# Forgetting attention on one Trainium2 core: scores from three split single-pass products instead of fp32 matmuls

## The reference, cut to what matters

```python
def forgetting_attention(q, k, v, f_pre, q_g, k_g):
    q = jnp.moveaxis(rms_norm_2(q, q_g), 1, 2)
    k = jnp.moveaxis(rms_norm_2(k, k_g), 1, 2)
    F = cumsum(log_sigmoid(f_pre))
    # for each block of 128 queries:
    logits = einsum('bhqd,bhkd->bhqk', q_blk, k) * Dh ** -0.5 + (F_q - F_k)
    logits = where(k_pos <= q_pos, logits, -inf)
    out = softmax(logits) @ v
```

## Time and profile before

| | |
|---|---|
| median of 3 runs | 1962.59 us (1961.63 to 1962.9) |
| the profiled execution | 1962.23 us |
| its span, first to last instruction | 1960.4 us |
| PE busy | 1946.3 us, 99% |
| VectorE, ScalarE, GpSimd busy | 45%, 39%, 31% |
| granted TensorE clock | 1.0 throughout |
| a pair of heads in the attention stage, from one to the next | 26.87 us (6 pairs in the steady rhythm) |

### The profile page before, as it was taken

The page is one execution under the profiler, slowest core; times in us unless marked ns, Lnnn a source line. Parts: engine busy times, 40 slices in busy tenths (PEclk is TensorE's granted clock), DMA queues, the critical chain, the costliest instruction groups (busy, mean ns, idle before and its releaser), DMA issues. The chain is left out here.

```text
span 1960.4 us, 26570 instructions
## 1 busy us (share of the span) xinstructions
PE 1946.3 (99%) x9186; PEld 1562.1 (80%) x9186; DVE 891.8 (45%) x1446; ACT 770.7 (39%) x1199; POOL 603.3 (31%) x238
## 2 busy tenths in 40 slices
PE   9999999999999999999999999999999999999999
PEld 7777888888888888888877887777788888888887
DVE  6888663344534544355274445555221364222200
ACT  7444442222222422222256556666422344222211
POOL 0000124444442344444403330000344423444443
PEclk9999999999999999999999999999999999999999
DMA  4111235555422455543212222222233333333322
GB/s 168 54 54 55 76 118 193 192 193 186 146 92 86 155 193 192 194 170 134 87 59 85 66 86 86 86 75 75 66 96 96 97 97 97 96 96 96 110 92 98
DMA packets 59271, 220.25 MB, mean 112 GB/s; under 512 B 6592, under 2 KB 7360, under 8 KB 59216
## 3 DMA queue, kind: packets, MB, share of 16 engines
q1 hardware_dynamic: 59216, 219.55, 34.0%
HBM read 217.39 MB, written 2.13 MB: 112 GB/s over the span
## 5 line engine op out<-in xcount | busy, mean ns | idle before, releaser
L438 POOL TENSOR_TENSOR wlo<-raw,whi 128x1024 fp32r<-128x1024 f32 (+1 forms) x234 | 603.0, 2577 | 1343.4 <-ACT whi L956 1343.4
L479 PE MATMUL bank<-xh,whi 128*128 128x512 f32 x1632 | 645.5, 396 | 3.5 <-DVE wlo L1512 3.3
L479 PE MATMUL bank<-xh,wlo 128*128 128x512 f32 x1632 | 635.8, 390 | 0.0
L479 PE MATMUL bank<-xl,whi 128*128 128x512 f32 x1632 | 635.5, 389 | 0.0
L956 ACT ACTIVATE whi<-raw 128x1024 fp32r<-128x1024 f32 (+1 forms) x298 | 330.2, 1108 | 604.4 <-PE bank L479 580.5
L479 PEld LDWEIGHTS bank<-xh,whi 128*128 128x128 f32 x1632 | 306.4, 188 | 81.4 <-issue 14.4
L479 PEld LDWEIGHTS bank<-xh,wlo 128*128 128x128 f32 x1632 | 306.3, 188 | 64.8
L479 PEld LDWEIGHTS bank<-xl,whi 128*128 128x128 f32 x1632 | 306.6, 188 | 62.3 <-issue 1.0
L479 PE MATMUL bank<-acth,whi 128*128 128x512 f32 x528 | 205.7, 390 | 1.4 <-POOL wlo L438 1.4
L1932 DVE SCALAR_TENSOR_TENSOR adaw<-adaw,crow 128x1024 f32<-128x1024 f32 x72 | 107.6, 1495 | 218.4 <-DMA adaw<-ada_dram 218.4
L479 PE MATMUL bank<-acth,wlo 128*128 128x512 f32 x528 | 205.4, 389 | 0.0
(11 more groups left out here) (314 smaller groups left out, 2017.1 us busy)
## 6 DMA issues: line engine op xcount, KB each, us to landing
raw<-w_dram SPq DMA_DIRECT2D x250, 512.0 KB, 3.6
adaw<-ada_dram SPq DMA_DIRECT2D x72, 512.0 KB, 4.3
raw<-wd_dram SPq DMA_DIRECT2D x48, 704.0 KB, 4.0
adaw<-w_dram SPq DMA_DIRECT2D x8, 512.0 KB, 4.4
norms<-fox_log_decays SPq DMA_DIRECT2D x8, 512.0 KB, 4.4
h<-x_dram SPq DMA_DIRECT2D x4, 512.0 KB, 6.9
out_dram<-h SPq DMA_DIRECT2D x8, 256.0 KB, 4.3
crow<-w_dram SPq DMA_DIRECT2D x2, 512.0 KB, 6.2
```

What stands on the lines that cost most here:

```text
L438: nc.gpsimd.tensor_tensor(wlo[:, s, 0:width], raw[:, s, 0:width], whi[:, s, 0:width].bitcast(F32), ALU.subtract).then_inc(sem("w_lo"), 1)
L479: mm = nc.tensor.matmul(proj[b][:], w[:, s, W], v[:, k, :], start=first and j == 0 and a == 0, stop=last and j == len(chunks) - 1 and a == ...
```

## The change

It does four things.

1. `fox_scores` computes scores from split operands. `fqq[:, e]` holds the high part of head e's queries twice, in both halves of the rows; `fkk[:, e]` holds the high part of its keys in its own half and the low part in the other half. One fp32r matmul over all 128 rows per head gives high-by-high plus high-by-low, and a second one over the head's 64 rows adds the low part of the queries (`fql`) by the high part of the keys. Low by low is left out. The mask is unchanged.
2. `fox_normed` writes its result over `fraw`. ScalarE makes the high parts in six copies of 64 partitions (`fox_high`), VectorE the low parts in four subtractions of 64 partitions (`fox_low`). `fox_high` stands in ScalarE's list between the roots and `split` of slab s+3. `f_qk` now counts six signals: four from VectorE and the two last copies of ScalarE.
3. The scores of the next pair's block 0 move behind chunks 3 to 6 of slab s+2 on PE; at the start they move behind two more chunks of slab 3.
4. On VectorE `weight_low` of slab s+3 moves from before the maxima of the next pair's block 0 to behind their scaling.

`fql` lies in the space of `gates_raw`, which is used earlier.

```diff
-        fq = sb("fq", [P, 2, S], F32, fox)
-        fk = sb("fk", [P, 2, S], F32, fox)
+        fqq = sb("fqq", [P, 2, S], F32R, fox)
+        fkk = sb("fkk", [P, 2, S], F32R, fox)
+        fql = low_part[:, 8:8 + S]
...
-        BESIDE = (((0, 0, 6),), ((0, 6, 8), (1, 0, 5)), ((1, 5, 8), (2, 0, 3)), ((2, 3, 8),))
+        BESIDE = (((0, 0, 6),), ((0, 6, 8), (1, 0, 5)), ((1, 5, 8), (2, 0, 3)), ((2, 3, 7), (2, 7, 8)))
...
                 if b == 0:
-                    pe.wait_ge(sem("f_qk"), primed(t * 2 + 2))
+                    pe.wait_ge(sem("f_qk"), primed(t * 6 + 6))
                 for e in range(2):
-                    H = slice(e * DH, e * DH + DH)
-                    nc.tensor.matmul(bank[2 + e][:, 0:W], fq[H, tt, b * P:W], fk[H, tt, 0:W], start=True, stop=False,
+                    nc.tensor.matmul(bank[2 + e][:, 0:W], fqq[:, e, b * P:W], fkk[:, e, 0:W], start=True, stop=False,
+                                     skip_group_check=True)
+                for e in range(2):
+                    H = halves(e)[0]
+                    nc.tensor.matmul(bank[2 + e][:, 0:W], fql[H, b * P:W], fkk[H, e, 0:W], start=False, stop=False,
                                      skip_group_check=True)
...
-                    elif more:
-                        fox_scores(t + 1, 1 - tt, 0)
...
+                            if (j, lo) == (2, 7):
+                                fox_scores(t + 1, 1 - tt, 0)
                             wide("fox", i, 6, s + j, part=(lo, hi))
...
-            wide("fox", 0, 6, 3, part=(0, 4))
+            wide("fox", 0, 6, 3, part=(0, 6))
             pe.wait_ge(sem("m_gated"), primed(MH * 2))
             fox_scores(0, 0, 0)
-            wide("fox", 0, 6, 3, part=(4, KC))
+            wide("fox", 0, 6, 3, part=(6, KC))
...
+            def fox_high(p):
+
+                act.wait_ge(sem("f_normed"), p * 2 + 1)
+                act.wait_ge(sem("scores"), p * 8 + UA)
+                for e in range(2):
+                    H = halves(e)[0]
+                    nc.scalar.activation(fkk[H, e, :], fraw[H, 1, :], ACT.Copy).then_inc(sem("f_hi"), 1)
+                act.wait_ge(sem("f_normed"), p * 2 + 2)
+                for e in range(2):
+                    H = halves(e)[0]
+                    nc.scalar.activation(fqq[H, e, :], fraw[H, 0, :], ACT.Copy).then_inc(sem("f_hi"), 1)
+                for e in range(2):
+                    H, O = halves(e)
+                    nc.scalar.activation(fqq[O, e, :], fraw[H, 0, :], ACT.Copy).then_inc(sem("f_qk"), 1)
...
                         fox_root(t + 1, 1)
                         fox_root(t + 1, 0)
+                        fox_high(t + 1)
                         split(i, 6, SLAB["fox"], s + 3, WC)
...
+            def fox_low(p):
+
+                for e in range(2):
+                    H, O = halves(e)
+                    dve.wait_ge(sem("f_hi"), p * 4 + (e + 1))
+                    V.tensor_tensor(fkk[O, e, :], fraw[H, 1, :], fkk[H, e, :].bitcast(F32), ALU.subtract).then_inc(sem("f_qk"), 1)
+                for e in range(2):
+                    H = halves(e)[0]
+                    dve.wait_ge(sem("f_hi"), p * 4 + (e + 3))
+                    V.tensor_tensor(fql[H, :], fraw[H, 0, :], fqq[H, e, :].bitcast(F32), ALU.subtract).then_inc(sem("f_qk"), 1)
...
                     for j in (1, 0):
                         fox_normed(t + 1, 1 - tt, j)
-                    weight_low(i, 6, s, 3)
+                    fox_low(t + 1)
                     fox_maxima(t + 1, 1 - tt, 0)
                     fox_maxima(t + 1, 1 - tt, 1)
                     fox_scale(t + 1, 0)
                     fox_scale(t + 1, 1)
+                    weight_low(i, 6, s, 3)
```

More of the change, by code:

```diff
@@ L114, in build @@
         leb = sb("leb", [P, P], BF16)
-        gates_raw = sb("gates_raw", [P, KC * 96])
+        grs = ExitStack()
+        gates_raw = sb("gates_raw", [P, KC * 96], F32, grs)
+        grs.close()
+        low_part = sb("low_part", [P, KC * 96], F32R)
         stat = sb("stat", [P, 2, 8])
@@ L1351, in fox_tile @@
                 matmuls(i * 6 + (SLAB["fox"] + s + 1))
-                act.wait_ge(sem("f_qk"), primed(p * 2))
+                act.wait_ge(sem("f_qk"), primed(p * 6))
                 bias = c1("b_fox", i * 6 + s)
@@ L1457, in _ @@
                 fox_root(0, j)
+            fox_high(0)
             fox_values(0, 2)
@@ L2169, in fox_normed @@
                 dve.wait_ge(sem("f_rstd"), p * 2 + (2 - j))
-                V.scalar_tensor_tensor((fq, fk)[j][:, par, :], fraw[:, j, :], c1(("fox_q", "fox_k")[j], p), frs[:, j, :], ALU.mult,
-                                       ALU.mult).then_inc(sem("f_qk"), 1)
+                V.scalar_tensor_tensor(fraw[:, j, :], fraw[:, j, :], c1(("fox_q", "fox_k")[j], p), frs[:, j, :], ALU.mult,
+                                       ALU.mult).then_inc(sem("f_normed"), 1)
+            def fox_low(p):
[7 more added lines that the diff above has]
+                    V.tensor_tensor(fql[H, :], fraw[H, 0, :], fqq[H, e, :].bitcast(F32), ALU.subtract).then_inc(sem("f_qk"), 1)
             def fox_pair(i, tt, more=True):
@@ L2201, in _ @@
                 fox_normed(0, 0, j)
+            fox_low(0)
             for k in range(2):
```

## The result

| | before | after |
|---|---|---|
| median | 1962.28 us (6 runs, 1961.45 to 1962.9) | 1971.93 us (6 runs, 1971.46 to 1973.84) |
| profiled execution | 1962.23 us | 1971.99 us |
| its span | 1960.4 us | 1970.2 us |

The ratio of the times is 1.0052, with a 95% interval from 1.0043 to 1.0062. The change makes the kernel 9.65 us slower: slower by more than 0.2%, as forecast, 1.5 us above the predicted time and within the range.

What follows compares the result with a forecast made beforehand. PE's list was taken as the bound, busy 1946.3 of 1960.4 us. From 1962.23, −3.5 (PE's gain) + 8.3 (stall) + 3.1 (first pair) gave 1970.1, against the median 1970.4 us, slower by 0.4%; range 1965 to 1974.

Steps and rivals of the forecast that it cites:

- The bound and the number on which it turns: PE's list bounds the kernel; `fox_values(t, 1)` starts 3.13 us after the block 3 `fpT` copies it needs.
- ScalarE's six copies: Ahead of split and `fpT` copies: 0.41 us wait plus six at 0.63, 3.78, making them 4.19 us later.
- The 0.12 that I added: Delay in us from the end of ScalarE's last `fpT` copy until PE sees it, at 1239.63.
- the stall's term: PE waits for `fpT` before the values, 1.18 us in each of 7 pairs: +8.3 us.
- No overlap between copies that change the half: Copies alternating partition half, like the two 64-partition squares, don't overlap on ScalarE: 0.63 us each.
- The threshold of that rival: Rival: copies overlap, 0.52 us each, sum +2.6, 1965.2 us, chance 0.12; below 0.57 a copy, not slower by 0.2%.
- PE's gain: Split scores shorten PE's list by 0.20, 0.15, 0.09 and 0 us per block, 0.44 per pair: −3.5 us.
- The sign that I named for it: In the profile after, scores at 512 columns take 0.95 us from first matmul to the next operation's load.
- Full-row loads: Rival: full-row weight loads of the score matmuls don't overlap, 0.22 us per block, +5.3: 1975.7 us; chance 0.03.
- Narrow `fp32r` matmuls: Rival: under 512 columns they run in four passes; 128 alone 1970.8 us, all three widths 1990, chance 0.04.
- Everything behind the stall: `f_qk` just in time; subtractions, exponentials, `weight_low` and slab s+3 stay covered, so nothing further is late.
- The first pair: Copies and later scores start the mask 3.1 us later, and the whole delay passes to the turned block: +3.1 us.

Runs made afterwards that it cites:

- e1: Kernel before plus six idle ScalarE copies of 64 partitions by 512 behind the roots of pairs 1 to 7: 1969.67 us, ratio 1.0038.
- e2: Changed kernel without its six copies and four subtractions, PE's matmuls the same in number, shape and order: 1960.8 us, ratio 0.9994.
- e5: Changed kernel with ScalarE's `fpT` copies and the evacuation ahead of the split of slab s+3: 1966.81 us, ratio 1.0025.
- e6: Changed kernel with the four query copies in another order of halves, query subtractions following it: 1971.9 us, ratio 1.0050.
- e9: Against kernel before: blocks 1 to 3 split by two 128-partition copies, half-row matmuls; block 0 fp32; first `weight_low` of slab 4 behind scalings: 1958.82 us, ratio 0.9985.
- e3: Changed kernel with the scores of the next pair's block 0 back at their old place on PE: 1999.06 us, ratio 1.0186.
- e4: Changed kernel with `weight_low` of slab s+3 back ahead of the maxima in VectorE's list: 1973.44 us, ratio 1.0056.

## Why the prediction was right, step by step

- **The bound and the number on which it turns.** PE's list, and 3.13 us of slack at `fox_values(t, 1)`. Confirmed from both sides: adding only the copies makes the stall (e1), taking them away (e2) or letting `fpT` pass the split (e5) removes it.
- **ScalarE's six copies, mis-sized by 0.23 a pair.** I took 0.63 each, 3.78; they are 0.655 apart (1236.98 to 1240.92 for six), 3.94 in all. The wait ahead of them is 0.48 where I had 0.41: the split started 1.04 behind the roots, the copies start 1.52 behind them. 3.13 of slack and these two give 1.31 instead of 1.06. The 0.12 that I added until PE sees the last copy stands in no row that the prediction names; it measured 0.05. V0 to V1 shows 1.34 to 1.42 in the five steady pairs, 1.63 in the first and 1.26 in the last, where I had 1.18 for all. In 7 pairs that is the 1.5 us by which the stall's term was too small.
- **No overlap between copies that change the half.** The reason that I gave held as well as the number. All five neighbours in the change differ in the half that they read or write, and none overlaps; the one pair of e6 that does not change it overlaps by 0.10. The Trainium skill's "ScalarE: Activation LUTs" (the paragraph on the ACTIVATE, under "What ACT_TABLE_LOAD costs") lets back-to-back ones overlap by about 93 ns, without a condition. This case's traces agree for the copies of 128 partitions in e9 (0.52 apart) and for that one pair of 64, and not where the half changes. The threshold of that rival was off: by the prediction's own terms the change is slower by under 3.9 us from below 0.55 us a copy, not 0.57.
- **PE's gain, 0.44 predicted, 0.36 measured.** The full-row matmuls follow the transpositions without a drain, but not at the spacing I took. In after the two start at 1229.826 and 1230.140, 0.31 apart, where I had 0.23: which I read as the first `fp32r` load behind a transposition not being hidden fully. From the last transposition (1229.80) to the values (1230.90) it is 1.10, predicted 1.06, before 1.26. The sign that I named for it, 0.95 from the first score matmul to the next load, came out at 1.07: the first matmul starts 0.03 behind the last transposition and not 0.11.
- **Full-row loads.** The rival that they don't overlap fell: the second one's load runs from 1229.909, during the first one's matmul, and the period of e2 is 26.51 where that rival wants over 27. The Trainium skill's "TensorE: Matmul & The Clock Gate" (Part 3, what overlaps) lets a load overlap only when its row group differs. These two loads take all rows, and the traces decide against it here.
- **Narrow `fp32r` matmuls.** Block 0's scores at 128 columns start 0.16 apart (1240.95, 1241.12): below the 0.21 that four passes would need; in e2, where both loads ran ahead, 0.06 apart (1237.37, 1237.43). That rival fell too.
- **Everything behind the stall.** `f_qk` was a little late rather than just in time (the wait row of L840, 3.1 us in 6 pairs, part of it a load's normal gap); it cost nothing in after because it lies in the stall, and e5 shows the 0.18. Exponentials, `weight_low` and slab s+3 kept their cover: PE comes to the turned block 1.67 us behind the first matmul of the values, before and after.
- **The first pair.** +3.1 predicted, +3.24 measured, passed on whole to the turned blocks (8.36 and 8.74 us behind the sums before, 11.60 and 11.99 after). e2 divides it: 1.4 is the position behind two more chunks, the other 1.8 the copies.

The predicted 1970.4 is 1.5 below the 1971.93 measured. The mis-sized terms are 1.5 (stall), 0.6 (gain) and 0.1 (first pair). All three miss to the same side. Against them stand, by chance, 0.4 by which this execution was ahead when it came to the attention stage, and 0.3 by which the median of before is lower over six runs than over the three that were shown.

## What to carry to other kernels

When work on the bounding engine is traded for work on an engine that is 39% busy, look where the new work stands in that engine's list: what it delays has a slack of its own, and here 4.4 us went ahead of an instruction with 3.1 us of slack. A split of the same operands in two copies costs nothing where it stands behind what PE waits for (e9). And count instructions before elements: a copy of 64 partitions takes as long as one of 128 (0.61 to 0.63 us), so a layout that needs half-partition copies pays double, and more where neighbours change the half and so lose the 0.1 us of overlap.

## What the runs showed of the hardware that was not expected

- Successive copies on ScalarE overlap by 0.1 us when both read and write the same partitions (0.52 us apart at 128 partitions in e9; the one such pair of 64 in e6, 0.10 of overlap), and not when the half that they read or the half that they write changes (0.64 to 0.66 apart, in after, e1 and e6).
- A wait of 2.75 us on TensorE was followed by some 8 matmuls at its level of 1.2 GHz, 0.42 us apart instead of 0.23: 1.6 us on top of the wait in the pair shown, and a mean period of 31.6 in which the wait alone would give 29.6 (e3; 26.51 of e2 and its mean wait of 3.05). Waits of 1.0 to 1.4 us in after had no such sequel. A wait of 1.6 us at the first pair had one in the profiled execution of e4 and none in those of after, e5 and e6; the first pair was 1.9 us longer there.
- The same fall shows outside the change. From about 1018.6 to 1021.2 us in the kernel before, and at nearly the same time in every other, PE has a hole of 2.6 us (it waits for the weights' low part from VectorE). In the profiled execution of before the two windows from 1016 to 1028 us have a clock of 1.00 and 1.00, in that of after 0.98 and 0.73. The clock fell there in five of the twelve profiled executions. It cost nothing that the traces show: from PE's start behind the hole to the first sum of squares it is 156.50 to 156.61 us in all twelve, with the fall and without.
